# Differential attention scores in two products in place of three, in a two-layer encoder on one Trainium2 core

## The reference

```python
def diff_attention(q, k, v, lam):
    ...
        sc = jnp.einsum("bqhcd,bkhcd->bchqk", qblk, k).astype(jnp.float32) * (dq ** -0.5)
        p = jax.nn.softmax(sc, axis=-1)
        a = p[:, 0] - lam * p[:, 1]
        return jnp.einsum("bhqk,bkhd->bqhd", a.astype(v.dtype), v)
```

## Time and profile before

| | us |
|---|---|
| three runs | 1196.32, 1197.32, 1197.56 |
| median | 1197.32 |
| the profiled execution | 1196.31 |
| its span (first to last instruction) | 1194.5 |

### The profile page before, as it was taken

One profiled execution on the slowest core, in us unless ns is written; L12 is line 12 of the kernel. 1 busy time (PEld: TensorE's weight loads), 2 busy tenths in 40 slices (PEclk: granted clock), 3 DMA queues, 4 the chain that ended last, 5 costly groups with the idle time before them and its releaser, 6 DMA issues.

```text
span 1194.5 us, 14513 instructions
## 1 busy us (share of the span) xinstructions
PE 1175.4 (98%) x5588; PEld 980.8 (82%) x5588; DVE 718.2 (60%) x837; ACT 567.5 (48%) x724; POOL 77.3 (6%) x129
## 2 busy tenths in 40 slices
PE   7999999999999999999999999999999999999997
PEld 5788888888888888788888888888888887888886
DVE  5376655566755945755656554565656557668554
ACT  5545453554555634564444435444344444445442
POOL 2400001000000000010000000000000001000000
PEclk9999999999999999999999999999999999999999
DMA  9986473554645555455555547474654646354541
GB/s 367 258 251 254 143 244 141 182 205 142 246 162 226 176 211 179 173 193 176 212 187 188 184 127 263 162 246 145 225 183 149 251 173 211 141 191 161 195 158 70
DMA packets 41894, 231.57 MB, mean 194 GB/s; under 512 B 7104, under 2 KB 7232, under 8 KB 16368
## 3 DMA queue, kind: packets, MB, share of 16 engines
q1 hardware_dynamic: 39120, 221.27, 52.9%
q0 software_dynamic: 1856, 7.38, 2.4%
q10 hardware_dynamic: 864, 2.18, 0.5%
HBM read 217.17 MB, written 2.10 MB: 184 GB/s over the span
## 4 chain that ended last, share of the span: by engine, by line
PE 93%; DMA 3%; DVE 1%; ACT 1%; SPq 1%; issue 1%; ACTq 0%; DVEq 0%
PE acc L429 84%; PE bank_x L569 2%; DMA probs<-x_nat 2%; PE bank_x L553 1%; PE bank_y L522 1%; DMA raw<-weights 1%; SPq L313 1%; ACT w_hi L676 1%; PE bank_y L511 1%; PE bank_x L565 1%; DVE w_lo L943 1%; PE bank_y L518 0%; PE bank_y L538 0%; PE bank_x L538 0%; PE bank_x L466 0%
## 5 line engine op out<-in xcount | busy, mean ns | idle before, releaser
L429 PE MATMUL acc<-w_hi,act_hi 128*128 128x512 f32 x1560 | 617.1, 396 | 2.8 <-DVE w_lo L943 2.8
L429 PE MATMUL acc<-w_lo,act_hi 128*128 128x512 f32 x1560 | 608.3, 390 | 0.0
L943 DVE TENSOR_TENSOR w_lo<-raw,w_hi 128x2048 fp32r<-128x2048 f32 x195 | 447.1, 2294 | 205.2 <-ACT w_hi L676 205.1
L676 ACT ACTIVATE w_hi<-raw 128x2048 fp32r<-128x2048 f32 x195 | 373.3, 1916 | 225.1 <-PE acc L429 201.1
L429 PE MATMUL acc<-w_hi,act_lo 128*128 128x512 f32 x1560 | 417.9, 390 | 0.1
L429 PEld LDWEIGHTS acc<-w_hi,act_lo 128*128 128x128 f32 x1560 | 292.6, 188 | 62.7 <-DVE act_lo L952 0.8
L429 PEld LDWEIGHTS acc<-w_hi,act_hi 128*128 128x128 f32 x1560 | 293.1, 188 | 61.3 <-DVE w_lo L943 3.3
L429 PEld LDWEIGHTS acc<-w_lo,act_hi 128*128 128x128 f32 x1560 | 293.2, 188 | 57.0
L683 ACT ACTIVATE unit<-acc,pre_r 128x512 f32<-128x512 f32 x78 | 49.3, 684 | 111.6 <-PE acc L429 111.2
L698 ACT ACTIVATE probs<-scores,negm 128x256 f32<-128x256 f32 (+1 forms) x80 | 36.7, 459 | 126.0 <-DVE negm L1034 99.5
L374 POOL TENSOR_TENSOR rope_c<-unit,cst 128x256 f32<-128x256 f32 (+1 forms) x19 | 15.8, 834 | 814.5 <-ACT unit L683 682.0
(11 more groups left out here) (166 smaller groups left out, 579.5 us busy)
## 6 DMA issues: line engine op xcount, KB each, us to landing
raw<-weights SPq DMA_DIRECT2D x195, 1024.0 KB, 4.8
qk_raw<-postg SPq DMA_DIRECT2D x176, 64.0 KB, 2.0
resid<-x_turned SPq DMA_DIRECT2D x8, 256.0 KB, 9.7
mix<-rpb POOLq DMA_DIRECT2D x32, 64.0 KB, 24.3
postg<-post_g POOLq DMA_DIRECT2D x2, 1024.0 KB, 8.2
resid<-x_perm POOLq DMA_DIRECT2D x2, 1024.0 KB, 8.9
out<-resid SPq DMA_DIRECT2D x8, 256.0 KB, 2.2
raw<-weights SPq DMA_DIRECT2D x2, 512.0 KB, 5.7
```

Of the source, the lines that this page charges most:

```text
L429: m = nc.tensor.matmul(tiles[t][:, :], a[:, kt, t * P:(t + 1) * P], w[:, buf, kk * NB:(kk + 1) * NB], start=(kt == 0 and a is act_hi and w ...
L676: nc.scalar.activation(w_hi[:, at % SPLIT, :], raw[:, at % RAW, :], ACT.Copy).then_inc(S["hi_ready"], 1)
L943: nc.vector.tensor_tensor(w_lo[:, at % SPLIT, :], raw[:, at % RAW, :], w_hi[:, at % SPLIT, :].bitcast(F32), ALU.subtract).then_inc(S["lo_r ...
```

## The change

Each map is made of two products over all 128 rows in place of three. For map c, the 64 rows of its own component (`mine`) hold the query's high part, and the 64 rows that were zero (`other`) hold the query's low part. The keys of component c are written to both halves of the rows, once as high part and once as low part (`both_k`). The product with the high keys gives high x high plus low x high, that with the low keys high x low plus low x low. `both_k` takes the room of `split_q`; the queries go to `q_hi`. POOL's clearing and the wait for it are gone. For the differential units ScalarE now splits at h = 1, and VectorE at h = 2 (map 0) and h = 4 (map 1). TensorE waits for `qk_ready` at each map, one count per map.

```diff
-        with nc.sbuf_tensor("split_q", [P, 2, 2, NT * UH, P], F32R) as split_q:
+        with nc.sbuf_tensor("both_k", [P, 2, 2, QUADS, NT * UH * QUAD], F32R) as both_k:
...
+        def hi_count(u):
+
+            return 2 * split_units(u) + (0 if u.kind == "A" else 2 * (u.index - 2) if u.kind == "B" else 4)
...
-                    if layer == 0 and u.index == 2:
-
-                        pool.wait_ge(S["masked"], 2 * UH)
-                        pool.memset(split_q[:, :, :, :, :].rearrange("p c b a n -> p (c b a n)").bitcast(F32), 0.0).then_inc(
-                            S["q_zeroed"], 1)
...
             def score_map(u, j, c):
+                pe.wait_ge(S["qk_ready"], 2 * split_units(u) + c + 1)
                 if c == 0:
-                    pe.wait_ge(S["qk_ready"], 2 * split_units(u) + 2)
                     if j > 0:
...
                 for t in range(NT):
-                    for n, (a, b) in enumerate(PARTS):
+                    for part in range(2):
                         m = nc.tensor.matmul((Y, X)[c][:, t * SEQ:(t + 1) * SEQ].rearrange("p (t a c) -> p t a c", t=NT, a=QUADS),
-                                             split_q[:, c, a, t * UH + j, :],
-                                             keys_of((k_hi[:, :, :], k_lo)[b], j), start=(n == 0), stop=(n == len(PARTS) - 1))
+                                             q_hi[:, c, t * UH + j, :], keys_of(both_k[:, c, part, :, :], j),
+                                             start=(part == 0), stop=(part == 1))
...
                 if u.kind == "B":
 
-                    act.wait_ge(S["q_zeroed"], 1)
                     for c in range(2):
-                        rows = slice(64 * c, 64 * c + 64)
-                        m = nc.scalar.activation(by_quads(split_q[rows, c, 0, :, :]), raw_quads(0, rows), ACT.Copy)
-                    m.then_inc(S["qk_hi"], 1)
+                        mine, other = (slice(64 * r, 64 * r + 64) for r in (c, 1 - c))
+                        nc.scalar.activation(by_quads(q_hi[mine, c, :, :]), raw_quads(0, mine), ACT.Copy).then_inc(S["qk_hi"], 1)
+                        nc.scalar.activation(both_k[other, c, 0, :, :], qk_raw[mine, :, 1, :], ACT.Copy)
+                        nc.scalar.activation(both_k[mine, c, 0, :, :], qk_raw[mine, :, 1, :], ACT.Copy).then_inc(S["qk_hi"], 1)
+                    return
...
-                if h == 2:
+                if h == (1 if u.kind == "B" else 2):
                     split_qk_hi(u)
...
+            def split_both_lo(u, c):
+
+                mine, other = (slice(64 * r, 64 * r + 64) for r in (c, 1 - c))
+                dve.wait_ge(S["qk_hi"], hi_count(u) + 2 * c + 1)
+                nc.vector.tensor_tensor(by_quads(q_hi[other, c, :, :]), raw_quads(0, mine),
+                                        by_quads(q_hi[mine, c, :, :].bitcast(F32)), ALU.subtract)
+                dve.wait_ge(S["qk_hi"], hi_count(u) + 2 * c + 2)
+                for rows in (other, mine):
+                    m = nc.vector.tensor_tensor(both_k[rows, c, 1, :, :], qk_raw[mine, :, 1, :],
+                                                both_k[mine, c, 0, :, :].bitcast(F32), ALU.subtract)
+                m.then_inc(S["qk_ready"], 1)
+
...
-                if h == 3 and u.kind != "G":
+                if u.kind == "B" and h in (2, 4):
+                    split_both_lo(u, h // 2 - 1)
+                if h == 3 and u.kind not in ("B", "G"):
                     split_qk_lo(u)
```

More of the change, by code:

```diff
@@ L234, in build @@
                  "y_sq y_scaled y_sum y_var y_std y_rdy "
-                 "rs_v rs_s rs_rdy tanh_done gate_u gate_done q_zeroed").split()
+                 "rs_v rs_s rs_rdy tanh_done gate_u gate_done").split()
         S = {n: sem(n) for n in names}
@@ L987, in turn_qk @@
                 m.then_inc(S["qk_turned"], 1)
+            def split_both_lo(u, c):
[8 more added lines that the diff above has]
+                m.then_inc(S["qk_ready"], 1)
             def split_qk_lo(u):
                 for blk in range(2):
[L993 to L999, removed]
+                    dve.wait_ge(S["qk_hi"], hi_count(u) + blk + 1)
+                    if blk == 0 or u.kind == "D":
                         m = nc.vector.tensor_tensor(by_quads(q_lo[:, blk, :, :]), raw_quads(blk),
```

## The result

The changed kernel takes 1208.9 us (median of 6 runs, 1205.4 to 1209.7) where the kernel before takes 1196.2 (6 runs, 1195.8 to 1197.6): ratio 1.0098, 95% interval 1.0088 to 1.0108, so about 1% slower. The forecast was slower by 0.7%, 1204.6 us, with a range up to 1208.5. The profiled execution took 1206.02 us, among the fastest of the six, against 1196.31 in the kernel before: 9.7 us to explain in the trace, and some 3 us more in the median, of which no trace was taken.

A forecast was written before the change was run, and what follows sets the result against it. TensorE was taken as the bound. Stalls at map 1 (3.4 and 4.15 us) plus two slow restarts (2.3 each) make 12.15, less 3.84 for products saved: +8.3, so 1204.6 us, range 1200.5 to 1208.5.

The forecast's parts named there:

- What bounds the kernel: TensorE, busy 98%, bounds nearly everywhere: a matmul less is time gained, a wait put before it is lost in full.
- The products: On TensorE, map products fall from 96 to 64; 32 at 0.12 us each gain 3.84 us.
- The new wait at map 1: TensorE stalls for map 1's low key parts from VectorE: 3.4 us in the first differential unit, 4.15 in the second.
- The clock: TensorE's clock falls in both map 1 gaps; each slow restart costs up to 2.3 us.
- Rival (a): Stalls at map 1 happen, but the clock stays up in one or both gaps: 1201.8 us, 1203.2 with one fall; chance 0.37.
- The second wait of 0.9: Before the turn of the probabilities, TensorE stalls 0.9 us more per unit at full clock; a slow restart swallows it.
- The sum for the two units: Both differential units: stalls and slow restarts of 12.15 us less 3.84 saved, +8.3 us.
- Rival (b): Key pieces on ScalarE and VectorE cost far less than taken, so not slower: 1195.7 us at half cost; chance 0.09.
- Rival (c): Writing one half's rows from the other costs extra on ScalarE and VectorE: +2.4 us on top, 1207.0; chance 0.07.

The follow-up runs named there:

- e8: Changed kernel with the second product of each map made twice, so three products again; 1207.8 us, ratio 1.0090.
- e6: Changed kernel with the differential units' heads two half-steps later and ScalarE's copies for map 1 behind the weight copy of chunk 3; 1195.8 us, ratio 0.9989.
- e12: The changed kernel run once more, unaltered, beside later runs; 1206.2 us, ratio 1.0083.
- e11: Changed kernel with 32 small 8x8 products added at the head of TensorE's program; 1206.9 us, ratio 1.0088.
- e3: Changed kernel with 14 products of 128x512 added on TensorE just ahead of its wait for map 1, in each differential unit; 1204.2 us, ratio 1.0066.
- e4: Changed kernel without the keys in the other half of the rows, POOL clearing the room as before; 1197.8 us, ratio 1.0009.
- e2: Changed kernel with ScalarE copying map 1's high parts at half-step 3, behind the weight copy of chunk 3; 1198.8 us, ratio 1.0018.
- e1: Changed kernel with VectorE making map 1's low parts at half-step 3, ahead of w_lo of chunk 3; 1200.4 us, ratio 1.0034.
- e5: Changed kernel with the four heads of the differential units two half-steps later; 1198.7 us, ratio 1.0011.
- e9: e6 with 32 small 8x8 products added at the head of TensorE's program; 1194.7 us, ratio 0.9993.
- e10: The kernel before with 96 small 8x8 products added at the head of TensorE's program; ratio 1.0034, 4.1 us slower by its median.

## Why the prediction was right

- **What bounds the kernel**: right. For 600 us between unit 3 and the last unit the two kernels keep step to 0.01 us; a wait of TensorE is lost in full.
- **The products**: 96 fell to 64. Two heads of unit 2, between the milestones at 250.37 and 277.88 before and 254.33 and 280.97 after, take 27.51 and 26.64 us: 0.87 for 8 products, 0.11 each, so 3.5 us in all; the same two heads of e8 (0.88 for 8) and unit 3 of e6 (1.75 for 16) say the same. The 3.84 of the text, 0.12 each from one map, was 0.3 too much.
- **The new wait at map 1**: right in place, order and mechanism, mis-sized by 0.4. Predicted 3.4 and 4.15 us, measured 3.78 and 4.51. The term is the spacing of the key copies on ScalarE: taken as 0.97, measured 1.07 to 1.09 (232.28, 233.36, 234.43), the upper bound of the text; w_hi of chunk 3 comes 6.48 us after the first copy, not 6.04. Two smaller terms nearly cancel: what follows w_lo on VectorE came 2.32 us behind its start, not 2.20, and TensorE resumed 0.06 us after the last piece, not 0.25. VectorE's three pieces were as taken (3.6 us, 243.03 to 246.63).
- **The clock**: right that both gaps bring a fall (in unit 3 it came 0.5 us behind the gap), which was the author's estimate from the one fall at the end of the run, 2.3 us after the work; too high in price. The first restart of the run gave 2.3 us as an upper end; measured 1.41 and 1.67. Rival (a) is out for this execution, and for e12 and e11, which have both falls too. The second wait of 0.9, which the fall was said to swallow, is not there when the clock falls, and is there (0.82, 0.77) when e3 keeps it up.
- **The sum for the two units**: 3.78 + 1.41 + 4.51 + 1.67 = 11.4 less 3.5 to 3.8 is 7.6 to 7.9; the milestones say 7.89, the text said 8.3. That is nearer than the terms are, and so in part luck: the two stalls were taken 0.7 too low together, the two restarts 1.5 too high, the products 0.3 too high.
- **Rival (b)**, cheap key copies: out. 64 rows with the keys laid evenly take 1.06 us, as 128 rows did (1.06). **Rival (c)**, dearer copies across halves: out; L724 and L725 both take 1.06, and the two key pieces of VectorE together 2.45.
- **What failed** is a sentence by silence: every part of the program that the change doesn't touch was taken to keep its time. The last unit lost 2.68 us in the profiled execution. 7.89 + 2.68, less the 0.75 of the start, make the 9.8 of the milestones (9.7 in the time). The median, 12.7 us up, lies 0.4 us over the range. Its four slowest runs have a granted clock of 0.989 to 0.992 over the run, the two fastest 0.994 and 0.995; that longer half-rate stretches make up the last 3 us is likely from this (e8 has one twice as long as the others), and was not shown, since no trace of such a run exists. In e12, later and beside the others, the same kernel took 1206.2 us, ratio 1.0083.

## What to carry to other kernels

When an edit doubles small pieces of preparation, ask not what they cost but which queue they stand in and what stands behind and ahead of them: here 7 us went with an order, and moving one block of three pieces ahead of, or three copies behind, the weight work of one chunk took most of it back. Read the total of an experiment by milestones along the run, not as one number: e8 looked like no change and was plus 4.1 and minus 2.7. And where the gain sought is about 0.3%, look for what the edit moves elsewhere by its mere number of instructions.

## What the runs showed of the hardware that was not expected

- One 16 KB packet of the queue that the profile names instruction, falling into a series of 16 small transfers of SyncE's queue, went with an issue of 10.4 to 11.4 us in place of 10.0 (25 of 26 such series), and 28 to 64 matmuls more or less on TensorE moved it from one gather to another.
- The clock fell to half 2.3 us after the last product of the run (its group ends at 1186.28 + 1.07 = 1187.35, and 0.62 over 1189.5 to 1190.0 puts the fall at 1189.6), 3.1 us after the work stopped in unit 2 (products end at 243.07, fall at about 246.2). In unit 3 the products ended at 323.29 and resumed at 327.64, and the granted clock fell only then, as its stretches show:

```profile
326.00:328.00 2.00, 0.36 (x3) 0.36 (x4) 1.96 (x3) 0.00 (x0) 0.00 (x0) 1.00 1.03 434
328.00:330.00 2.00, 2.00 (x8) 1.63 (x7) 1.97 (x3) 1.02 (x4) 0.00 (x0) 0.53 0.02 8
330.00:332.00 2.00, 2.00 (x7) 1.61 (x6) 1.47 (x3) 0.46 (x2) 0.00 (x0) 0.62 0.24 41
```

  0.53 over 2 us puts the fall at about 328.1, 0.5 us after the work was back. A gap that is over can still be paid for. TensorE's idle time in these two gaps was 3.62 and 4.35 us.
- Shorter gaps were followed by a fall as well: those ahead of the last unit's maps of 1.98 us (e6), 2.13 (e4), 2.20 (e2), 2.22 (e1), 2.25 (changed kernel) and 2.47 (e5), and the waits near 45 us of 2.06 (e6), 2.23 (e1), 2.66 (e9), 2.87 (e11) and 4.27 (e10). Gaps of 1.91 us (e10), 1.70 (e5) and 1.59 (e12) were not.
- Products added in a gap made the kernel faster in those units (e3), by 0.95 us for two gaps.
